# Early first weights, norms through PSUM, residual tiles shared with GpSimd, and keys in half banks, in a two-block transformer kernel

## The reference, cut to what matters

```python
def rms_norm(x, gain=None):
    y = xf * lax.rsqrt(jnp.mean(xf * xf, axis=-1, keepdims=True) + EPS)
...
h = rms_norm(x, norm_mix[l]);  proj = h @ w_in[l]
...
h = rms_norm(x, norm_x[l]);    q = h @ xq[l];  k, v = split(m @ xkv[l])
...
h = rms_norm(x, norm_ffn[l])
...
_modnorm(x, g_pre, shift, scale) = _rmsnorm(x, g_pre) * (1 + scale) + shift
_residual(x, y, g_post, gate, weight) = x + weight * gate * _rmsnorm(y, g_post)
```

## Time and profile before

| what | value |
|---|---|
| median of 3 runs | 2490.72 us (2489.73 to 2495.57) |
| profiled execution, its own time | 2487.36 us |
| its span, first to last instruction | 2485.5 us |
| TensorE busy with matmuls | 2352.1 us, 95% |
| VectorE, ScalarE, GpSimd busy | 36%, 35%, 45% |
| mean granted TensorE clock | 0.981 |

### The profile page before, as it was taken

How to read it: one execution, slowest core, us unless ns; L and a number is a source line. 1 busy time by engine, 2 the same in 40 slices (tenths; PEclk the granted TensorE clock), 3 DMA queues, 4 the chain that set the end, 5 groups by cost and what they waited for, 6 DMA issues and landing times.

```text
span 2485.5 us, 33338 instructions
## 1 busy us (share of the span) xinstructions
PE 2352.1 (95%) x11994; PEld 1909.4 (77%) x11994; DVE 901.4 (36%) x1528; ACT 873.4 (35%) x1239; POOL 1108.8 (45%) x1344
## 2 busy tenths in 40 slices
PE   5999998889999999999999999999999998999997
PEld 4778677567888878888888878877867885878885
DVE  3334623376868672111111044243134445111114
ACT  3344534443323343211211234255434534322222
POOL 3434355166989773433333333333331043555553
PEclk8999999989999999999999999999999998999998
DMA  3222132145555541121111121122220021222222
GB/s 129 94 76 77 68 102 86 69 144 189 199 178 197 187 142 64 55 68 65 64 62 66 60 77 66 69 89 75 77 89 26 1 85 51 102 93 97 98 94 93
DMA packets 66602, 231.35 MB, mean 93 GB/s; under 512 B 7216, under 2 KB 9520, under 8 KB 66352
## 3 DMA queue, kind: packets, MB, share of 16 engines
q1 hardware_dynamic: 50224, 179.36, 21.3%
q10 hardware_dynamic: 16256, 50.21, 6.0%
HBM read 226.66 MB, written 2.10 MB: 92 GB/s over the span
## 4 chain that ended last, share of the span: by engine, by line
issue 51%; POOL 34%; PE 14%; DVE 1%; POOLq 1%; DMA 0%; ACT 0%; DVEq 0%; ACTq 0%; SPq 0%
POOL WLO L317 34%; PE ps L1668 11%; PE ps L1686 3%; POOLq L270 0%; DVE X L1374 0%; DVE TN L1370 0%; POOLq L315 0%; DMA RAW<-in_stream_dram 0%; DVE Y L1396 0%; PE ps L1737 0%; POOLq L317 0%; DVE TN L1018 0%; DVE Y L1394 0%; DVE GLO L1259 0%; ACT RS L742 0%
## 5 line engine op out<-in xcount | busy, mean ns | idle before, releaser
L317 POOL TENSOR_TENSOR WLO<-RAW,WHI 128x256 fp32r<-128x256 f32 x1340 | 1108.6, 859 | 1349.2 <-ACT WHI L341 1348.2
L341 ACT ACTIVATE WHI<-RAW 128x1024 fp32r<-128x1024 f32 x335 | 354.4, 1058 | 696.4 <-DMA RAW<-in_stream_dram 677.3
L1668 PE MATMUL ps<-HLO,WHI 128*128 128x512 f32 (+2 forms) x1368 | 456.6, 367 | 9.1 <-DVE XK L1191 2.5
L1668 PE MATMUL ps<-HHI,WHI 128*128 128x512 f32 (+2 forms) x1368 | 448.7, 361 | 0.0
L1668 PE MATMUL ps<-HHI,WLO 128*128 128x512 f32 (+2 forms) x1368 | 448.5, 361 | 0.0
L1668 PEld LDWEIGHTS ps<-HLO,WHI 128*128 128x128 f32 (+1 forms) x1368 | 236.9, 188 | 56.7 <-issue 5.1
L1668 PEld LDWEIGHTS ps<-HHI,WHI 128*128 128x128 f32 (+1 forms) x1368 | 236.9, 188 | 43.5 <-issue 3.6
L1668 PEld LDWEIGHTS ps<-HHI,WLO 128*128 128x128 f32 (+1 forms) x1368 | 237.1, 188 | 40.9
L1254 DVE TENSOR_TENSOR SF<-SF,ps 128x512 f32<-128x512 f32 (+1 forms) x66 | 51.3, 777 | 541.7 <-PE ps L1668 378.3
L1686 PE MATMUL ps<-HHI,WHI 128*128 128x512 f32 (+1 forms) x584 | 206.7, 383 | 36.0 <-POOL WLO L317 24.8
L1668 PE MATMUL ps<-GLO,WHI 128*128 128x512 f32 (+1 forms) x704 | 232.2, 365 | 4.8 <-POOL WLO L317 2.4
(11 more groups left out here) (364 smaller groups left out, 3083.2 us busy)
## 6 DMA issues: line engine op xcount, KB each, us to landing
RAW<-in_stream_dram SPq DMA_DIRECT2D x335, 512.0 KB, 3.3
ADA<-in_ada_dram ACTq DMA_DIRECT2D x72, 512.0 KB, 4.0
BM<-in_bias_dram ACTq DMA_DIRECT2D x8, 448.0 KB, 3.8
DECAY<-in_decay_dram ACTq DMA_DIRECT2D x4, 512.0 KB, 4.4
out_dram<-X SPq DMA_DIRECT2D x8, 256.0 KB, 2.0
X<-in_x_dram SPq DMA_DIRECT2D x2, 512.0 KB, 5.8
X<-in_x_dram ACTq DMA_DIRECT2D x2, 512.0 KB, 6.7
C<-in_mem_dram ACTq DMA_DIRECT2D x1, 1024.0 KB, 5.5
```

The costliest lines, as they stand in the source:

```text
L317: op = nc.gpsimd.tensor_tensor(WLO[:, slot(u), k:k + 2], RAW[:, slot(u), k:k + 2], WHI[:, slot(u), k:k + 2].bitcast(F32), ALU.subtract)
L341: nc.scalar.activation(WHI[:, j], RAW[:, j], ACT.Copy).then_inc(unit_hi, 1)
L1668: mm = nc.tensor.matmul(out, w, x[:, k, tok], start=(k == 0 and n == 0), stop=(k == kt - 1 and n == 2))
```

## The change

- The start: the first two weight units are issued ahead of const and vec, and SyncE issues COS, SIN and LAMV too, behind the four units. n1's squares are summed on VectorE, with one matmul (sum_of) at the end. ScalarE converts units 0 and 1 right behind the squares, unit 2 behind tile 3's copy; the two small matrices are copied behind tile 7's. Factor (bank 7) and TN (banks 3, 4) lie in PSUM.
- n2, n3 and a4 also have the factor and TN in PSUM (`factor`, `scaled`).
- p1, p3 and p5 (`post`): even tiles stay on VectorE through PSUM; of an odd tile VectorE makes the product in SBUF, and GpSimd adds it to X (`odd_tiles`, 128 x 512), in its queue between the units of `lows`. Who waits for a tile asks `tile_at`.
- Keys 4 to 7 lie in halves of banks 2 and 3, since n2 takes banks 4, 5 and 6. For that key_unit(5) and key_unit(7) wait for the square of the key before (xk_sq), key_unit(6) waits for w_out_x, the sum of keys 4 and 5 for n2's Exp and no longer for its Ln, and xq's third unit is followed by the wait for all keys.
- A wait of TensorE for the factor before a4's sums, and one behind them, are gone.

In the diff, "..." stands for unchanged lines; the removed helpers `root` and `sums` are left out too.

```diff
...
-XK_BANKS = (5, 6, 5, 6, 2, 3, 5, 6)
+XK_BANKS = ((5, 0), (6, 0), (5, 0), (6, 0), (2, 0), (2, 256), (3, 0), (3, 256))
...
-NORMS = [("n1", KD, _to_h), ("nm", KD, _acc), ("n2", KD, _acc), ("n3", KD, _acc), ("a0", KD, _acc), ("p1", KD, _to_x),
-         ("a1", KD, _to_h), ("ckv", 2, _to_h), ("cq", 6, _to_h), ("p3", KD, _to_x), ("a4", KD, _to_h), ("p5", KD, _to_x)]
+NORMS = [("n1", KD, _acc), ("nm", KD, _acc), ("n2", KD, _acc), ("n3", KD, _acc), ("a0", KD, _acc), ("p1", KD, _to_x + ("px",)),
+         ("a1", KD, _to_h), ("ckv", 2, _to_h), ("cq", 6, _to_h), ("p3", KD, _to_x + ("px",)), ("a4", KD, _to_h), ("p5", KD, _to_x + ("px",))]
...
-        (SQP, ACCP, SQA, SQC, ACCC), _ = region(
+        (SQP, ACCP, SQA, SQC, ACCC, TNP), _ = region(
...
-            ("ACCC", [P, M], F32))
+            ("ACCC", [P, M], F32), ("TNP", [P, 2, S], F32))
...
+                    if kind in ("x", "px"):
+                        tiles = KD // 2
...
+        def tile_at(tag, k):
...
+            return norm_at(tag, "px" if k % 2 else "x", k // 2 + 1)
...
+        def key_bank(j, n=M):
...
+            bank, c0 = XK_BANKS[j]
+            return ps[:, bank, c0:c0 + n]
...
-            sp.dma_start(vec[:], t["vec"]).then_inc(const_landed, 16)
-            sp.dma_start(const[:], t["const"][:, 0:7 * P].rearrange("p (c n) -> p c n", n=P)).then_inc(const_landed, 16)
...
+                if u == 2:
+                    sp.dma_start(const[:], t["const"][:, 0:7 * P].rearrange("p (c n) -> p c n", n=P)).then_inc(const_landed, 16)
+                    sp.dma_start(vec[:], t["vec"]).then_inc(const_landed, 16)
...
+            sp.dma_start(COS[:], t["const"][:, 7 * P:7 * P + S]).then_inc(s("ret_tables"), 16)
+            sp.dma_start(SIN[:], t["const"][:, 7 * P + S:7 * P + 2 * S]).then_inc(s("ret_tables"), 16)
+            sp.dma_start(LAMV[:].rearrange("p a n -> p (a n)"), t["lam"].partition_broadcast(P).rearrange("p o n -> p (o n)")).then_inc(s("lam_landed"), 16)
...
-                sp.wait_ge(*norm_at("p5", "x", k + 1))
+                sp.wait_ge(*tile_at("p5", k))
...
-            lows(0, UNITS)
+            def odd_tiles(tag, tn):
...
+                for k in range(1, KD, 2):
+                    pool.wait_ge(*norm_at(tag, "p", k + 1))
+                    nc.gpsimd.tensor_tensor(X[:, k], X[:, k], tn(k // 2), ALU.add).then_inc(s("norm_px"), 1)
...
+            lows(0, UNIT["na_q"])
+            odd_tiles("p1", lambda j: TNP[:, j % 2])
+            lows(UNIT["na_q"], UNIT["ffn2"] + AHEAD)
+            odd_tiles("p3", lambda j: TN2[:, j % 2, 0:S])
+            lows(UNIT["ffn2"] + AHEAD, UNITS)
+            odd_tiles("p5", lambda j: TN3[:, j % 2, 0:S])
...
+            def factor(tag, bank, out=None, n=1):
...
+                act.wait_ge(*norm_at(tag, "ms", n))
+                nc.scalar.activation(ps[:, bank], ps[:, bank], ACT.Ln, scale=1.0 / D, bias=eps).then_inc(s("norm_ln"), 1)
+                act.wait_ge(*norm_at(tag, "ln", 1))
+                nc.scalar.activation(ps[:, bank if out is None else out], ps[:, bank], ACT.Exp, scale=-0.5).then_inc(s("norm_rs"), 1)
...
-            act.wait_ge(const_landed, 32)
+            for k in range(KD):
+                act.wait_ge(x_landed[k // 2], 16)
+                square("n1", SQ, k, k, [(X[:, k], 0, S)])
+            convert(0)
+            convert(1)
...
+            act.wait_ge(*norm_at("n1", "ms", 1))
+            nc.scalar.activation(ps[:, 7], ps[:, 7], ACT.Ln, scale=1.0 / D, bias=eps).then_inc(s("norm_ln"), 1)
+            act.wait_ge(*norm_at("n1", "ln", 1))
+            nc.scalar.activation(ps[:, 7], ps[:, 7], ACT.Exp, scale=-0.5).then_inc(s("norm_rs"), 1)
+            for k in range(KD):
+                act.wait_ge(*norm_at("n1", "t", k + 1))
+                nc.scalar.activation(HHI[:, k, 0:S], ps[:, 3 + k % 2], ACT.Copy).then_inc(s("norm_hi"), 1)
+                if k == 3:
+                    convert(2)
...
-            norm("n1", lambda k: X[:, k], KD, S, D, RS, SQ, TN, dst=HHI, ready=lambda k: act.wait_ge(x_landed[k // 2], 16),
-                 between=lambda k: convert(k) if k < AHEAD else None)
...
-                nc.scalar.activation(sq_key[:, j % 2], ps[:, XK_BANKS[j], 0:M], ACT.Square).then_inc(s("xk_sq"), 1)
+                nc.scalar.activation(sq_key[:, j % 2], key_bank(j), ACT.Square).then_inc(s("xk_sq"), 1)
...
-                nc.scalar.activation(HHI[:, k, 0:S], TN[:, k % 2], ACT.Copy).then_inc(s("norm_hi"), 1)
+                nc.scalar.activation(HHI[:, k, 0:S], ps[:, 5 + k % 2], ACT.Copy).then_inc(s("norm_hi"), 1)
...
-            act.wait_ge(*norm_at("n2", "ms", 1))
-            nc.scalar.activation(RS[:, 0, 0:S], ps[:, 7], ACT.Ln, scale=1.0 / D, bias=eps).then_inc(s("norm_ln"), 1)
-            act.wait_ge(*norm_at("n2", "ln", 1))
-            nc.scalar.activation(RS[:, 0, 0:S], RS[:, 0, 0:S], ACT.Exp, scale=-0.5).then_inc(s("norm_rs"), 1)
+            factor("n2", 7, 4)
...
-            norm("n3", None, KD, S, D, RS, SQ, TN, dst=HHI)
+            factor("n3", 7)
+            for k in range(KD):
+                act.wait_ge(*norm_at("n3", "t", k + 1))
+                nc.scalar.activation(HHI[:, k, 0:S], ps[:, 4 + k % 2], ACT.Copy).then_inc(s("norm_hi"), 1)
...
-            root("p1", 6)
+            factor("p1", 6)
...
-                act.wait_ge(*norm_at("p1", "x", k + 1))
+                act.wait_ge(*tile_at("p1", k))
...
-            root("a1", 4)
+            factor("a1", 4, n=KD)
...
-            norm2("p3", KD, None, S, D, None, RS2, TN2, None)
-            norm2("a4", KD, [(lambda k: X[:, k], 0, S)], S, D, SQ2, RS2, TN2, lambda k: act.wait_ge(*norm_at("p3", "x", k + 1)), HHI, shift(6))
+            factor("p3", 6)
+            for k in range(KD):
+                act.wait_ge(*tile_at("p3", k))
+                if k >= 2:
+                    act.wait_ge(*norm_at("a4", "ms", k - 1))
+                nc.scalar.activation(SQ2[:, k % 2, 0:S], X[:, k], ACT.Square).then_inc(s("norm_sq"), 1)
+            factor("a4", 4, n=KD)
+            for k in range(KD):
+                act.wait_ge(*norm_at("a4", "t", k + 1))
+                nc.scalar.activation(HHI[:, k, 0:S], ps[:, (5, 7)[k % 2]], ACT.Identity, bias=mod[:, 6 * KD + k, 0:1]).then_inc(s("norm_hi"), 1)
...
-            norm2("p5", KD, None, S, D, None, RS3, TN3, None)
+            factor("p5", 6)
...
+            clear(TN[:, 0])
+            for k in range(KD):
+                add_square("n1", TN[:, 0], SQ, k, k)
...
-            norm("n1", lambda k: X[:, k], KD, S, lambda k: col("norm_mix", k), RS, TN, HHI, HLO)
...
+            def mix_low(k):
...
+                dve.wait_ge(*norm_at("n1", "hi", k + 1))
+                V.tensor_tensor(HLO[:, k, 0:S], ps[:, 3 + k % 2], HHI[:, k, 0:S].bitcast(F32), ALU.subtract).then_inc(s("norm_lo"), 1)
...
+            dve.wait_ge(*norm_at("n1", "rs", 1))
+            for k in range(KD):
+                if k >= 2:
+                    dve.wait_ge(*norm_at("n1", "lo", k - 1))
+                V.scalar_tensor_tensor(ps[:, 3 + k % 2], X[:, k], col("norm_mix", k), ps[:, 7], ALU.mult, ALU.mult).then_inc(s("norm_t"), 1)
+                if k:
+                    mix_low(k - 1)
+            mix_low(KD - 1)
...
-                    op = V.scalar_tensor_tensor(XK[:, 2 * g + j], ps[:, XK_BANKS[2 * g + j], 0:M], col("xk_gain", j),
+                    op = V.scalar_tensor_tensor(XK[:, 2 * g + j], key_bank(2 * g + j), col("xk_gain", j),
...
-            norm("n2", lambda k: X[:, k], KD, S, lambda k: col("norm_x", k), RS, TN, HHI, HLO,
-                 between=lambda k: key_scale(2) if k == 4 else None)
...
+            def scaled(tag, gain, rs, tns, bias=None, between=None):
...
+                def low(k):
+                    dve.wait_ge(*norm_at(tag, "hi", k + 1))
+                    if bias is None:
+                        V.tensor_tensor(HLO[:, k, 0:S], ps[:, tns[k % 2]], HHI[:, k, 0:S].bitcast(F32), ALU.subtract
+                                        ).then_inc(s("norm_lo"), 1)
+                    else:
+                        V.scalar_tensor_tensor(HLO[:, k, 0:S], ps[:, tns[k % 2]], bias(k), HHI[:, k, 0:S].bitcast(F32),
+                                               ALU.add, ALU.subtract).then_inc(s("norm_lo"), 1)
...
+                dve.wait_ge(*norm_at(tag, "rs", 1))
+                for k in range(KD):
+                    if k >= 2:
+                        dve.wait_ge(*norm_at(tag, "lo", k - 1))
+                    V.scalar_tensor_tensor(ps[:, tns[k % 2]], X[:, k], gain(k), ps[:, rs], ALU.mult, ALU.mult).then_inc(s("norm_t"), 1)
+                    if k >= 1:
+                        low(k - 1)
+                    if between:
+                        between(k)
+                low(KD - 1)
...
+            dve.wait_ge(s("xk_q"), 2)
+            scaled("n2", lambda k: col("norm_x", k), 4, (5, 6), between=lambda k: key_scale(2) if k == 4 else None)
...
-            norm("n3", lambda k: X[:, k], KD, S, lambda k: col("norm_ffn", k), RS, TN, HHI, HLO)
```

(69 more changed lines are left out.)

13 lines of the change are left out of this document (removed).

## The result

The changed kernel was timed twice, each time beside the kernel before on the same chip. First: 2469.07 us (median of 4) against 2493.14, ratio 0.9902, 95% interval 0.9887 to 0.9916. Later, unchanged, as r_after_again: 2465.17 (median of 4) against 2495.56, ratio 0.9876, interval 0.9860 to 0.9892. So it is faster, by 24 us in one sample and 30 in the other. The forecast of 2463.0 against 2490.72 is a ratio of 0.9889, between the two. The profiled execution took 2465.88 us (before 2487.36).

A forecast was written before the change was run, and what follows sets the result against it. TensorE, busy 95% of the span, was taken as the bound, so only its idle time and slow clock could go. Terms 16.1 + 4.9 + 0.1 + 3.6 + 1.4 + 1.5 = 27.6 off 2490.7 gave 2463 us, range 2457 to 2470.

The forecast's parts named there:

- Start: 16.1: Up to ret_value(0): new load order, earlier factor and converts let it start 16.1 us earlier; bounds 13 and 17.
- rival 1: At the start: const lands late behind the weights, so the start gives less and the total is 2468; chance 12%.
- n2 and keys: 4.9: At n2 and cross-attention's keys: PSUM operands speed DVE and GpSimd, gaining 4.9 us; bounds 2.0 and 5.7.
- rival 2: Between stages: new waits eat the gain, slow clock stays, n2 gives 2.5 and p1 2.6; total 2466.5; chance 10%.
- A GpSimd tile: 1.42: In p1, p3 and p5: a 128 x 512 addition on GpSimd takes 1.42 us, not over 2.35.
- rivals 3, 4 and 5: GpSimd tile costs 2.35 (7%); tile and DVE's next product don't overlap (3%); tile far dearer, kernel slower than before (2%).
- p1 to a1: 3.6: From p1 to a1: four fewer DVE additions and half the slow clock gain 3.6 us; bounds 1.5 and 4.9.
- p3 to a4: 1.4: From p3 to a4: odd residual tiles on GpSimd gain 1.4 us, same pattern as p5; bounds 0.3 and 1.8.
- eight matmuls behind it that keep up: At p3 to a4: TensorE's eight matmuls behind the tiles keep up, within the 1.4 us term.
- p5: 1.5: At p5: odd tiles on GpSimd cut 11.2 us to 9.8, with Ln and Exp 1.5 gained; bounds 0.5 and 1.7.
- Nothing else: All other stages: no further cost; behind each stage TensorE is the bound again, so a gain stays one.
- rival 5: At the odd tiles: GpSimd's tile is far dearer, deciding from 3.8 us a tile; at 5 us 2503; chance 2%.

The follow-up runs named there:

- e_start: The kernel before with the start alone changed (first loads' order, n1's squares on VectorE, PSUM, early converts); its ratio gives 16.5 us.
- e_keys: The kernel before with n2, the keys of cross-attention and n3 alone changed; its ratio gives 4.5 us.
- f_sq6: The changed kernel with the square of key 6 ahead of the root of keys 4 and 5 and the convert on ScalarE; 2.0 us gained by load 64.
- f_nav: The changed kernel with the first two na_v converts put behind the fifth and sixth square of C on ScalarE; 4.4 us further ahead by load 212.
- g_both: The changed kernel with na_v's two converts earlier and key 6's square ahead of convert and root; ratio 0.9882 to the kernel before.
- f_pads: The changed kernel with 40 unused semaphore increments in TensorE's stream in front of ffn0; the stall came in full, unit 80 landing after 5.77 us.
- g_ada: The changed kernel with ADA loads in ffn0's first loop issued in twos behind the second convert; its median is the changed kernel's.
- r_start_again: The kernel before with the start alone changed, executed a second time unchanged; fifteen ffn1 units took 124.8 us, against 127.3 in its first execution.
- h_short_dots: The changed kernel with the dot products of ADA and c cut from 1024 to 16 columns (values wrong); 2444.9 us, 20 under the changed kernel.

## Why the prediction was right, point by point

- **Start: 16.1, measured 16.75, 15.56** (16.15 in e_start). Landings, squares, factor, lows and pair came within 0.5 us of the forecast, the pair within 0.3. The factor did not wait for const, so rival 1 is out. WLO took 726 to 744 ns in the start and 714 to 752 at n2, VectorE's products up to 0.76, as said.
- **n2 and keys: 4.9, measured 4.4** in both traces and in e_keys. The new wait was found in advance, with its size (2.2). 3.4 us of slow clock followed it with TensorE busy throughout, which costs 1.7 us, where I had the slow clock "mostly" gone: that covers the missing 0.5. f_sq6, without that stretch, gains 5.7 up to the same load. With n2 at 4.4 and p1 at 3.9, rival 2 (2.5 and 2.6) is out.
- **A GpSimd tile: 1.42, measured 1.27 to 1.30.** Taking twice 0.732 less a fixed part was too little off. Beside it VectorE's product took 0.74, so they overlap and rivals 3, 4 and 5 fall. The Trainium skill's rule in "GPSIMD Engine Reference", section 4.1 (elementwise work on a tile goes to VectorE, GpSimd is about 2x slower on two inputs), holds in its ratio (1.27 against 0.69) and does not decide, as argued.
- **p1 to a1: 3.6, measured 3.9 and 3.8 at the first product of na_q**, half of the slow clock gone. By load 212 r_after_again still has 3.8 of it, the profiled run 2.4. The collision that the Trainium skill describes in "SBUF — State Buffer", section "Who interferes with whom" (a VectorE instruction with two SBUF inputs beside a GpSimd one that reads SBUF), is there. Four additions to ACCP, min/median/max:

```profile
L1544 DVE TENSOR_TENSOR ACCP<-ACCP,SQP x4: 418/764/1299, 1472.2 to 1475.0; 128x256 f32<-128x256 f32 x4
```

  Before, the four took 418 to 426. The second one started at 1472.74 and ended 0.28 behind GpSimd's tile (1472.38 to 1473.76), much as an exclusive lock would have it, though 0.28 is less than the 0.42 that it needs by itself, and GpSimd's tile took 1.38 instead of 1.27. As said, nobody on the path waited for it.
- **p3 to a4: 1.4, measured 0.1 to 0.25** in most traces. From p3's sum to the first product of ffn2 the kernel before took 19.58 us, the profiled run 19.33, r_after_again and f_nav 19.46, g_both 18.06. The term that was wrong is "eight matmuls behind it that keep up". TensorE's sums of the eight squares, of f_nav and of g_both:

```profile
2065.07 10.83 PE L2414 MATMUL ps<-SQ,const 128*128 128x512 f32 x16 [3.61 <-ACT SQ L1007]
```
```profile
2066.29 9.48 PE L2414 MATMUL ps<-SQ,const 128*128 128x512 f32 x16 [3.61 <-ACT SQ L1007]
```

  At a granted clock of 0.50 a tile's two matmuls take 1.7 to 2.0 us, more than the 1.39 between two tiles before, and the squares wait for them. In f_nav the slow clock covers the first 6.4 us of the row, in g_both 3.3. Like with like, the edit gives 1.5 where the stretch is 6.8 us long (g_both against before) and 0.6 to 0.7 where it is 10.2 (the others against e_keys' 20.07, which has the old p3).
- **p5: 1.5, measured 1.6 and 1.7**: from 2451.90 to 2461.5, 9.6 where 9.8 was forecast and the earlier trace rows has 11.2.
- **"Nothing else" is the step that failed.** It said that TensorE is the bound again behind each stage, so a gain stays one. Not in ffn0, where GpSimd's lows are the bound, and have been one before: a weight that lands 2.5 us late there costs TensorE 6 to 7 us. On the way to it 0.7 us were lost in the profiled run (0.44 of them a wait for XP on ScalarE, which e_start and e_keys have too), 1.6 in r_after_again. Not at na_v either. TensorE arrived there 19.3 us earlier than before and ScalarE's converts of na_v 17.2, behind the squares of C; the 17.2 are all gains up to p1, the 2.1 beyond them a faster clock over na_q's products. TensorE waited 2.70 and then ran 3.4 us at half clock, so that more than the 2.1 was gone; f_nav gave it back. I listed "if TensorE waits for WLO after p1" among what would make it wrong, but had looked for that wait in GpSimd's queue, not in ScalarE's, and not in the kernel before, which has it (0.63).
- **The sum** of 27.6 lies between 24 and 30. The edits' own stages add to about 27 in the profiled run (16.75, 4.4, 3.9, 0.25 and 1.6), so the mechanism of the start, which is the bulk, and of n2, p1 and p5 is right in size. That the total came out so near is in part luck, since things that the profile of one execution can't show run both ways: the stall, the spacing in ffn1, and the clock at the scores of latent attention. There the profiled run gained 3.5 us (2.9 more than r_after_again) that no edit earned, as the windows of before and after show (length, busy us and count of PE, PEld, DVE, ACT, POOL, then granted clock):

```profile
1881.00:1887.90 6.90, 6.10 (x21) 4.78 (x22) 2.09 (x6) 3.33 (x6) 0.00 (x0) 0.51 0.00 0
```
```profile
1865.50:1872.40 6.90, 6.88 (x47) 5.69 (x48) 2.81 (x8) 3.62 (x7) 0.00 (x0) 1.00 0.00 0
```

- **Two sums of the forecast** are off without effect on it: the best bounds add to 31.2, not 31.6, and rival 5 decides from 4.0 us a tile (2.2 + 4g is then 7 over 11.2), not from 3.8.

## What to carry to other kernels

Behind a gain, ask of each later stage which engine's queue order is the next bound, ScalarE's converts too, not only whether its wait list names TensorE's partner. Before two profiled executions are compared stage by stage, look at a second execution of the same kernel: here single stages moved by 3 to 6 us between two traces of one program, as much as an edit. And where one engine's work slows another's beside it, as VectorE's dot products of two SBUF tiles do GpSimd's lows here, look there first: leaving most of those products out gave 20 us, more than any single wait on the list. That is an upper bound of the prize and not a gain at hand, since the products have to be made somewhere, and 2.4 of it were VectorE's own time.

## What was not expected of the hardware

- TensorE's matmuls in ffn1 have two spacings, 124.8 and 127.3 us for fifteen units (2%), at a granted clock of 1.00 and with no idle time. It changes only where a chunk starts and holds through the chunk. What picks it stays open.
- After a wait of 2.73 us at the scores of latent attention the clock stayed at its upper level in the profiled run, e_keys, f_pads and g_ada, fell for 3.4 us in r_start_again and h_short_dots, and for 6.8 in g_both. The slow stretch behind one and the same short wait has no fixed length in these traces, so a forecast can only give it a chance.
- GpSimd's subtractions beside VectorE products of two SBUF tiles took up to 1.78 us each, 2.4 times the undisturbed 0.73, and a VectorE addition beside a GpSimd tile up to 1.30 instead of 0.42.
